# Forming the low half of a filler weight behind four masks, and loading the residual x tile by tile

## What is computed

```python
h = rms_norm(x, norm_mix)
u = h @ w_in                                   # RWKV, attention (FoX) and gate columns
o_r = rwkv_time_mix(u_r, ...)                  # a state carried through all positions
o_f = attention(q, k, v, log_forget)
merged = sigmoid(g_r) * (o_r @ w_br_rwkv) + sigmoid(g_f) * (o_f @ w_br_fox)
x = x + merged @ w_out                         # the residual x
x = x + square(relu(rms_norm(x) @ w_ffn_up)) @ w_ffn_down
y = rms_norm(x)
```

## Time and profile before

| | before |
|---|---|
| three runs, median (lowest to highest) | 2137.5 us (2125.45 to 2142.78) |
| the profiled execution | 2131.06 us |
| its span in the profile | 2129.2 us |
| PE busy | 2043.7 us, 96% |
| DVE, ACT, POOL busy | 943.1 us (44%), 617.1 us (29%), 194.6 us (9%) |
| mean clock granted to PE | 0.987 |
| moved by DMA | 185.36 MB, 87 GB/s |

### The profile page before, as it was taken

The page is one execution under the profiler, slowest core; times in us unless marked ns, Lnnn a source line. Parts: engine busy times, 40 slices in busy tenths (PEclk is TensorE's granted clock), DMA queues, the critical chain, the costliest instruction groups (busy, mean ns, idle before and its releaser), DMA issues.

```text
span 2129.2 us, 43171 instructions
## 1 busy us (share of the span) xinstructions
PE 2043.7 (96%) x17718; PEld 1836.3 (86%) x17718; DVE 943.1 (44%) x1507; ACT 617.1 (29%) x997; POOL 194.6 (9%) x186
## 2 busy tenths in 40 slices
PE   7999989999999999998899999999999999999997
PEld 7996678888888887665566999999999999999997
DVE  6557554444444454607685753332123222222334
ACT  5015332322232222214354642322022012202313
POOL 0000222222222222001110000000000000000000
PEclk9999999999999999999999999999999999999999
DMA  4214621111222202746644561111111111111112
GB/s 168 89 30 167 203 54 44 43 33 45 54 64 74 73 29 75 187 98 251 204 157 162 190 223 47 40 50 49 40 50 40 50 45 43 49 39 50 41 48 81
DMA packets 112938, 185.36 MB, mean 87 GB/s; under 512 B 65198, under 2 KB 68590, under 8 KB 111238
## 3 DMA queue, kind: packets, MB, share of 16 engines
q1 hardware_dynamic: 110502, 174.91, 26.2%
q10 hardware_dynamic: 2304, 8.50, 1.5%
HBM read 147.71 MB, written 35.67 MB: 86 GB/s over the span
## 4 chain that ended last, share of the span: by engine, by line
PE 84%; DVE 6%; DMA 4%; SPq 2%; issue 2%; ACT 1%; ACTq 0%; DVEq 0%
PE ps L292 47%; PE ps L385 10%; PE ps L996 4%; PE ps L997 3%; PE ps L381 3%; PE ps L382 2%; PE ps L383 2%; DMA weights<-in_wu 1%; PE ps L1027 1%; SPq L805 1%; DVE arena L1870 1%; PE ps L872 1%; DMA normed<-in_vp 1%; DVE arena L2036 1%; PE ps L1239 1%
## 5 line engine op out<-in xcount | busy, mean ns | idle before, releaser
L292 PE MATMUL ps<-h_high,wb_split 128*128 128x350 f32 x1536 | 290.5, 324 | 0.0
L292 PE MATMUL ps<-ff_high,wb_split 128*128 128x350 f32 x1488 | 281.0, 323 | 0.0
L302 ACT CAST wb_split<-weights 128x1024 fp32r<-128x1024 f32 x88 | 92.1, 1046 | 600.6 <-PE ps L292 592.9
L292 PEld LDWEIGHTS ps<-h_high,wb_split 128*128 128x128 f32 x1536 | 254.7, 189 | 0.4
L292 PEld LDWEIGHTS ps<-ff_high,wb_split 128*128 128x128 f32 x1488 | 247.2, 189 | 0.0
L385 PE MATMUL ps<-normed,weights 128*128 128x350 f32 x696 | 229.1, 477 | 0.0
L385 PEld LDWEIGHTS ps<-normed,weights 128*128 128x128 f32 x696 | 130.3, 194 | 67.7 <-issue 7.3
L2194 DVE TENSOR_TENSOR arena<-arena,ps 128x1050 f32 (+1 forms) x39 | 48.7, 1249 | 314.1 <-PE ps L292 314.1
L2277 POOL TENSOR_TENSOR arena<-arena,constants 64x512 f32<-64x512 f32 x120 | 132.7, 1106 | 386.9 <-DVE arena L1870 325.9
L292 PE MATMUL ps<-ff_low,wb_split 128*128 128x350 f32 x744 | 160.3, 323 | 0.0
L996 PEld LDWEIGHTS ps<-arena 64*64 64x64 f32 x2400 | 145.0, 135 | 16.7 <-issue 15.7
(11 more groups left out here) (329 smaller groups left out, 3406.8 us busy)
## 6 DMA issues: line engine op xcount, KB each, us to landing
weights<-in_wu SPq DMA_DIRECT2D x122, 512.0 KB, 3.5
normed<-in_vp SPq DMA_DIRECT2D x64, 260.0 KB, 4.7
normed<-in_kp SPq DMA_DIRECT2D x64, 256.0 KB, 5.6
arena<-chunk_dram SPq DMA_DIRECT2D x10, 1248.0 KB, 6.9
arena<-gate_dram SPq DMA_DIRECT2D x16, 525.0 KB, 4.1
chunk_dram<-arena SPq DMA_DIRECT2D x12, 520.0 KB, 5.0
chunk_dram<-fox SPq DMA_DIRECT2D x12, 520.0 KB, 4.6
arena<-samp_dram SPq DMA_DIRECT2D x10, 512.0 KB, 9.5
```

What stands on the lines that cost most here:

```text
L292: last = pe.matmul(PS[:, 3 * s + g, 0:G], ws[s][wh][:, k * P:(k + 1) * P], tile_of(x[xh], k)[:, g * G:(g + 1) * G], start=(k == 0 and wh + ...
L302: act.copy(of[0][s][0], W[:, s]).then_inc(w_hi[s], 1)
```

## The change

Two edits that have nothing to do with each other. In `dve_chunk` the low part of side 1 is formed behind the four masks and not ahead of them; nothing is added or removed. On SP the transfer of x is cut into its eight tiles of 525 KB, each issued right after the gate tiles of the same number, and DVE waits for all eight.

```diff
             gates_back(0)
             reload(V_BR0 + 1, 1)
+            x_tile(0)
             sp.wait_ge(sg_ready, 2)
             gates_back(1)
+            x_tile(1)
             with sp.Fori(2, KT) as n:
                 reload(n + V_BR0, 0)
                 reload(n + V_BR0, 1)
                 sp.wait_ge(sg_ready, 2 * n)
                 gates_back(n)
-            sp.dma_start(XT, A["xt"]).then_inc(x_back, 16)
+                x_tile(n)
...
                 done(dve.tensor_copy(Vn[0:C], PS[0:C, 3, :]), "nat_v")
-                if early:
-                    fill_split_low(dve, c, 1)
                 cm = cst[...]
                 for i in range(2):
                     for m, dst, bank in (("k", MK, 4), ("b", MB, 0)):
...
                             cm, ALU.mult), f"mask_{m}{i}")
+                if early:
+                    fill_split_low(dve, c, 1)
                 wait(ch_pool, "bm_0_low")
...
-            dve.wait_ge(x_back, 16)
+            dve.wait_ge(x_back, 16 * KT)
```

More of the change, by code:

```diff
@@ L842, in _, with x_tile @@
             sp.wait_ge(o_done, 2)
+            def x_tile(n):
+                sp.dma_start(XT[:, n, :] if isinstance(n, int) else
+                             XT[:, bass.ds(n, 1), :].rearrange("p o n -> p (o n)"),
+                             A["xt"][:, n, :] if isinstance(n, int) else
+                             A["xt"][:, bass.ds(n, 1), :].rearrange("p o n -> p (o n)")).then_inc(x_back, 16)
             gates_back(0)
             reload(V_BR0 + 1, 1)
+            x_tile(0)
             sp.wait_ge(sg_ready, 2)
             gates_back(1)
+            x_tile(1)
             with sp.Fori(2, KT) as n:
```

## The result

The changed kernel takes 2108.9 us (median of five runs, 2105.06 to 2115.49), the kernel before 2136.4 us (2125.45 to 2142.78) beside it. The ratio is 0.9886, with a 95% interval of 0.9846 to 0.9925: faster by 1.1%, and by at least 0.75%. The forecast was 2107.5 us.

The account below looks back on a forecast made before the run. PE, busy 96% of the span, was taken as the bound, so only its waits and slow clock pay. Masks 8.5, clock falls 8.1 and x 7.0 sum to 23.6 us off 2131.1: 2107.5 us, range 2100 to 2121.

Parts of the forecast that it names:

- Masks, 8.5 us: Chunks 1 to 9: masks start 0.94 us earlier, cutting PE's wait from 1.55 to 0.61 us; 8.5 us gained.
- Cover of the low part: Between `mask_b1` and `xt_init`: the low part's 1.03 us fits DVE's 2.33 us idle time, 1.3 us to spare.
- Falls, 8.1 us: Behind the masks, chunks 5 to 9: five drops of PE's clock to 0.50, 1.6 us each, vanish; 8.1 us.
- x, 7.0 us: End of branch stage: PE's 4.72 us wait and 2.31 us of half clock in the first output unit go.
- The price of a tile, 1.5 to 1.8 us, hidden: Branch stage: seven weight units land 1.5 to 1.8 us later behind a tile, hidden in 2.87 us of room.
- a fall at another link of the chunk: Sign of being wrong: the clock falling elsewhere in a chunk than behind the masks; no size given.
- masks that bring nothing: Rival, chunks: low part slows POOL's level masks, PE waits at `xt_init`; only 7.0 us gained, 2124.1 us; chance 0.09.
- tiles that hold the queue for 4.1 us or longer: Two rivals, branch stage: 4.1 us a tile, 2113.7 us, chance 0.08; 8.3 us a tile, 2143.1 us, chance 0.04.
- the falls stay: Rival, behind the masks: clock falls remain; 2115.6 us with five, 2122.1 with nine; chance 0.17.

Follow-up runs that it names:

- low part behind `xt_init`: Changed kernel with the low part of side 1 moved one step further down, behind `xt_init`: 2111.4 us, ratio 0.9878.
- x behind the weights: Changed kernel with x again one 4200 KB transfer, issued behind the first two weight units of the output projection: 2111.7 us, ratio 0.9900.
- x only: Kernel before with x loaded one tile at a time, the low part still ahead of the masks: 2126.0 us, ratio 0.9974.
- the full wait: Changed kernel with an unread DVE reduction of 850 constants ahead of the masks in chunks 1 to 9: 2127.5 us, ratio 0.9955; three executions profiled.
- masks only: Kernel before with the low part behind the masks, x still in one transfer behind the loop: 2117.3 us, ratio 0.9947.
- x in one turn: Changed kernel with all eight tiles of x issued in one turn of the branch stage, behind gates_back(4): 2116.3 us, ratio 0.9890.

## Why the forecast was right, point by point

- **Masks, 8.5 us.** Right. Chunks without a fall went from 59.82 to 58.87 us, 0.95 by nine chunks is 8.5. Chunk 0 of the kernel before gave the remaining wait (0.61 us) exactly.
- **Cover of the low part.** Right in sign, wrong in size. DVE's gap ahead of `xt_init` is 0.76 us and not 1.3: the second instruction of the low part took 1.50 us where it had taken 0.42. That an instruction grows beside the other engine's could be read before: the forecast took it as harmless that POOL's masks run beside `xt_init`, but of the four in the earlier trace rows the third, which starts 0.05 us behind `xt_init`, takes 1.78 us where the first takes 1.28:

```profile
370.01 1.78 POOL L2277 TENSOR_TENSOR arena<-arena,constants 64x512 f32<-64x512 f32 x1
```

  The cover that counts was elsewhere and larger: `xt_init` is done at 370.56, and PE takes it at 372.51.
- **Falls, 8.1 us.** All five went, four between chunks 1 and 9 (13.98 less 8 x 0.95 is 6.4) and one in chunk 9. The reason given, the length of the wait, is borne out as a condition, not as a rule: at 1.55 us it brought none to five falls in nine chunks. So the term was right for the execution that was profiled, and would have been another for another one; that it also served for the median is in part luck. The medians differ by 27.5 us, of which 9 x 0.95 + 4.72 = 13.3 us are waits removed; the other 14 us are, by subtraction, time at half the clock. This half depends on the chip. Two kernels that remove the same waits leave 14 us for it on one chip (low part behind `xt_init`, 2139.0 to 2111.4 us) and 4 us on another (x behind the weights, 2129.2 to 2111.7 us).
- **x, 7.0 us.** Measured 6.82 in the whole stage. The turns still take 11.59 us (1223.47 to 1235.06 in ACT's rows for the split of L302, as 1227.07 to 1238.66 before).
- **The price of a tile, 1.5 to 1.8 us, hidden.** Right for the transfer, undersized in all. A weight unit behind a tile lands 5.3 to 6.8 us after its issue and not 5.14, so up to 1.7 us later; but SP also issues it 0.57 us later in the turn, which the forecast set beside the transfers. In the turn where it is 1227.62 + 6.8 = 1234.4, ACT takes it at 1235.06:

```profile
1234.07 1.08 ACT L1678 ACTIVATE arena<-arena 128x1050 f32<-128x1050 f32 x1
1235.06 1.03 ACT L302 CAST wb_split<-weights 128x1024 fp32r<-128x1024 f32 x1
```

   Of the 2.87 us of room 0.6 is left. Tiles of 1050 KB would not have been hidden by this count; that wasn't tried.
- **Not foreseen.** A fall at 294.8 us costs 1.61 us: PE waits there for DVE's `fill_low`, by the same lengths as before, but with no fall before. The forecast had named a fall at another link of the chunk as a sign of being wrong. This one can't be laid to the edit: up to this place both kernels run the same instructions, since chunk 0 forms no low part. Of the twelve executions with the same instructions up to here, eight have it and four don't (before, x only, x behind the weights, the third with the full wait); why is open. The second is a single wait in the gates:

```profile
908.13 4.09 PE L385 MATMUL ps<-normed,weights 128*128 128x350 f32 x13 [1.21 <-DMA weights<-in_wu]
```

   It isn't the change's either: masks only, x behind the weights and x in one turn have 176.78 to 176.85 us from chunk 9 to attention, 2.5 us under the kernel before, which is chunk 9's mask and fall, and this execution has 178.26. The first execution with the full wait has the same wait in the gates, and the second, of the same kernel, doesn't (179.21 and 177.74 us). Against both stand 1.24 us that attention took less and 0.51 us ahead of chunk 0. That the forecast came within 1.4 us of the median owes something to luck: these four cancel in part (+1.6, +1.5, -1.2, -0.5).

Of the rivals, masks that bring nothing and tiles that hold the queue for 4.1 us or longer are refuted by the rows above. That the falls stay was right in its ground, that the condition isn't known, and wrong for waits of 1.09 us and less.

## What to carry to other kernels

Order within one engine's queue is free speed where the next engine waits for only one of the two neighbours: look for a short, late-needed instruction ahead of one that TensorE waits for, and for a long transfer ahead of a short one that is needed first. A stage that already exists without the disturbing work, like chunk 0 here, gives the size of the gain before any run. And where a loop's small waits bring the clock down in some executions, shortening them pays in two ways: by the medians a quarter to a half of this gain came from the clock, depending on the chip, and it is also the part that one profile sizes worst.

## What the hardware showed

**DVE and POOL hold each other up.** POOL's first level mask takes 1.28 us alone, and 1.78 us where DVE's low part began 0.05 us ahead of it; DVE's second instruction, begun during that mask, takes 1.50 us and not 0.42. POOL's timeline, before and then after:

```profile
367.71 1.28 POOL L2277 TENSOR_TENSOR arena<-arena,constants 64x512 f32<-64x512 f32 x1 [9.17 <-DVE arena L1870]
```

```profile
367.04 1.78 POOL L2285 TENSOR_TENSOR arena<-arena,constants 64x512 f32<-64x512 f32 x1 [8.23 <-DVE arena L1876]
```

The Trainium skill's page SBUF — State Buffer, in SBUF: two separate sides, says that VectorE with two inputs in SBUF and GpSimd share a pair of ports, which the one that starts first keeps for its whole instruction. The rows agree to about 0.2 us: POOL loses 0.50 us, while DVE's first instruction had 0.64 us left (366.99 + 0.69 - 367.04), and DVE's second ends at 369.10, 0.28 us behind POOL's mask (367.04 + 1.78 = 368.82). In the kernel with the low part behind `xt_init`, beside a mask that POOL had begun, DVE's first grows to 1.65 us and its second to 1.09. It cost no time here, as PE had room at both places; moved beside a busy POOL, an instruction of DVE is not the size that it has in its old place.

**The same wait brings half the clock in one execution and not in another.** Three executions of one kernel with waits of 1.56 us had 0, 0 and 1 falls in nine chunks each, the kernel before five. Each fall costs about 1.6 us, and at this wait every chunk after the first fall had one too.
